# Four reorderings and two blocks of constant matmuls in the two-layer part of a fused Trainium2 kernel

## What is computed

```python
h = rms_norm_2(x, norm_pre)
proj = h @ w_in
y_sb = flat(stick_breaking(heads(sb_q), heads(sb_k), heads(sb_v)))
h_ml = mlstm(...); y_ml = flat(head_norm(h_ml)) * sigmoid(ml_o)
y_gm = spatial_gating(gelu(gm_u), gelu(gm_v), ...)
y_rt = flat(head_norm(retention(rotary(rt_q), rotary(rt_k), rt_v)))
y_xa = flat(memory_attention(heads(xa_q), heads(mem_k), heads(mem_v)))
ys = stack([y_sb*silu(sb_z), y_ml*silu(ml_z), y_gm*silu(gm_z), y_rt*silu(rt_z), y_xa*silu(xa_z)])
up = einsum('bsnw,nwd->bsnd', ys, w_up)
merged = sum(sigmoid(gates) * up, axis=branches)
return x + rms_norm_2(merged @ w_out, norm_post)
```

## Time and profile before

| | |
|---|---|
| median of 3 runs | 2201.73 us (2200.91 to 2202.25) |
| the profiled execution, own time | 2199.61 us |
| its span, first to last instruction | 2197.8 us |
| TensorE busy | 1866.3 us, 85% of the span |
| VectorE busy | 1035.7 us, 47% |
| ScalarE busy | 407.9 us, 19% |
| mean granted clock of TensorE | 0.942 of full |
| moved by DMA | 595.02 MB, mean 271 GB/s |

### The profile page before, as it was taken

The page is one execution under the profiler, slowest core; times in us unless marked ns, Lnnn a source line. Parts: engine busy times, 40 slices in busy tenths (PEclk is TensorE's granted clock), DMA queues, the critical chain, the costliest instruction groups (busy, mean ns, idle before and its releaser), DMA issues. The chain is left out here.

```text
span 2197.8 us, 27405 instructions
## 1 busy us (share of the span) xinstructions
PE 1866.3 (85%) x11528; PEld 1162.8 (53%) x11528; DVE 1035.7 (47%) x1612; ACT 407.9 (19%) x787; POOL 0.2 (0%) x4
## 2 busy tenths in 40 slices
PE   8999977758666667766667999989999999989998
PEld 5687733323323333322223897874446898874445
DVE  7858522212112122122222768678663557768662
ACT  1123300000000000000001233223323233223322
POOL 0000000000000000000000000000000000000000
PEclk9999998888988888888998999999999999999999
DMA  7222899999999999999998334454533334454430
GB/s 307 81 77 102 342 434 429 431 430 432 430 431 429 433 430 430 431 429 430 430 433 348 144 130 159 142 222 153 188 121 136 143 127 169 134 194 193 160 147 19
DMA packets 32375, 595.02 MB, mean 271 GB/s; under 512 B 3966, under 2 KB 5248, under 8 KB 7560
## 3 DMA queue, kind: packets, MB, share of 16 engines
q1 hardware_dynamic: 30344, 584.31, 64.7%
q10 hardware_dynamic: 1920, 9.09, 1.3%
HBM read 590.22 MB, written 1.06 MB: 269 GB/s over the span
## 5 line engine op out<-in xcount | busy, mean ns | idle before, releaser
L2289 PE MATMUL ps<-ring,arena 128*32 128x512 f32 x2032 | 285.9, 714 | 156.3 <-DMA ring<-in_w_experts 147.6
L897 PE MATMUL ps<-ring,arena 128*128 128x512 f32 x656 | 286.4, 592 | 0.0
L2289 PEld LDWEIGHTS ps<-ring,arena 128*32 128x32 f32 x2032 | 72.0, 128 | 354.6 <-issue 219.3
L897 PEld LDWEIGHTS ps<-ring,arena 128*128 128x128 f32 x656 | 124.3, 190 | 155.0 <-issue 155.0
L2323 PE MATMUL ps<-ring,arena 128*32 128x256 f32 x2016 | 151.2, 450 | 62.8 <-DMA ring<-in_w_experts 62.1
L713 PE MATMUL ps<-arena,ring 128*128 128x128 f32 x1536 | 183.2, 275 | 2.7 <-issue 1.8
L713 PEld LDWEIGHTS ps<-arena,ring 128*128 128x128 f32 x1536 | 177.3, 192 | 5.4 <-issue 4.0
L2953 DVE COPY arena<-ps 128x256 f32<-128x256 f32 x64 | 27.2, 425 | 273.0 <-PE ps L2323 273.0
L713 PE MATMUL ps<-early,ring 128*128 128x128 f32 x1152 | 137.3, 275 | 2.9 <-DVE ring L1557 2.9
L2323 PEld LDWEIGHTS ps<-ring,arena 128*32 128x32 f32 x2016 | 70.5, 126 | 130.0 <-issue 76.6
L713 PEld LDWEIGHTS ps<-early,ring 128*128 128x128 f32 x1152 | 133.3, 192 | 4.5 <-DVE ring L1557 3.3
(11 more groups left out here) (476 smaller groups left out, 2471.8 us busy)
## 6 DMA issues: line engine op xcount, KB each, us to landing
ring<-in_w_experts SPq DMA_DIRECT2D x88, 4096.0 KB, 23.4
ring<-in_w_layers SPq DMA_DIRECT2D x64, 2048.0 KB, 7.8
ring<-in_w_experts SPq DMA_DIRECT2D x13, 2048.0 KB, 13.4
ring<-in_w_first SPq DMA_DIRECT2D x9, 2048.0 KB, 8.3
early<-in_w_layers SPq DMA_DIRECT2D x6, 2048.0 KB, 7.9
arena<-in_w_mem SPq DMA_DIRECT2D x4, 2048.0 KB, 20.1
ring<-in_w_first SPq DMA_DIRECT2D x4, 512.0 KB, 7.3
early<-in_w_experts SPq DMA_DIRECT2D x1, 2048.0 KB, 25.2
```

The costliest lines, as they stand in the source:

```text
L897: last = pe.matmul(ps[:, bank, :], lhs[:, k, :], rhs[:, k, :], start=(first and k == 0), stop=(k == n - 1), skip_group_check=True)
L2289: last = pe.matmul(ps[CAP * e:CAP * (e + 1), v // 4, :], xg[:, (v % 4) * 2 + k, CAP * e:CAP * (e + 1)], w[:, k, e, :], start=(v % 4 == 0 a ...
```

## The change

- SyncE waits for `in_turned` (both transfers of the rotation landed) before it issues the load of gm_u, in each layer.
- A helper `hold_clock` multiplies the constant matrix of ones by itself, n matmuls of 128x128 into a PSUM bank that nobody reads: 6 behind the last group of experts (bank 0), 2 ahead of layer 0 and 13 ahead of layer 1 (bank 7).
- TensorE's wait for `gm_mix` moves into the loop over the sb heads, behind `run(2)` and the wait for `sb_sp` of head 0.
- VectorE centres ml_v right behind the bound of the ml exponentials, ahead of `run(3)`.
- In the merge, the additions of g22 and u22 and the bound of g22 form `second_sums`. In branch 0 it stands ahead of the sums of the next branch's weights, in the others behind them as before. The bound of g22 now follows the addition of u22 in all five.

```diff
@@ layers_sync @@
                     if i >= RING2:
                         unit_end(i - RING2)
+                        if UNITS[i] == "gm_u":
+                            sp.wait_ge(sem("in_turned"), 32 * (l + 1))
@@ layers_pe @@
+        def hold_clock(pe, bank, n):
+            for _ in range(n):
+                pe.matmul(ps[:, bank, 0:P], ones, ones, start=True, stop=True)
...
+                hold_clock(pe, 7, 13 if l else 2)
                 unit_in(plan.unit_at["gm_v"])
...
                 sb_logits(1)
                 evacuated(pe, job("sb_v", 1))
-                w("gm_mix", 4, 4)
                 for hd in range(NH):
                     run(2)
                     w("sb_sp", NH, hd + 1)
+                    if hd == 0:
+                        w("gm_mix", 4, 4)
@@ layers_dve @@
                 dve.tensor_scalar(wide_flat, wide_flat, 1e18, None, ALU.min).then_inc(sem("ml_qkm"), 1)
+                centre_values("ml_v", ml_v, ml_sum, "ml_vc")
                 run(3)
...
                 run(2)
                 gate_bound("ml_o")
-                centre_values("ml_v", ml_v, ml_sum, "ml_vc")
                 run(2)
...
+                def second_sums(b):
+                    add_product(b, 1, g22, G_BANK[2], "gate_prod", "gate_c", "gate_q")
+                    add_product(b, 1, u22, U_BANK[2], "up_prod", "up_c", "up_q")
+                    bound(b, 1, g22)
...
+                    if b == 0:
+                        second_sums(b)
                     if b + 1 < NBR:
                         gate_difference(b + 1)
                         gate_total(b + 1)
                         up_sums(b + 1)
-                    add_product(b, 1, g22, G_BANK[2], "gate_prod", "gate_c", "gate_q")
-                    bound(b, 1, g22)
-                    add_product(b, 1, u22, U_BANK[2], "up_prod", "up_c", "up_q")
+                    if b:
+                        second_sums(b)
                     gather(b, 1, merged[:, 1, HALF:D], g22, u22)
@@ end of the first part, TensorE @@
             expert_group(pe.snap(more_rounds * NGRP + NGRP - 1), tail=True)
+            hold_clock(pe, 0, 6)
```

More of the change, by code:

```diff
@@ L1539, in layers_dve, with centre_values @@
                     dve.tensor_tensor(y, y, ps[:, 5, 0:SEQ], ALU.mult).then_inc(sem("xa_y"), 1)
+                def centre_values(name, v, sums, done):
+                    for m in range(2):
+                        evacuated(dve, job(name, m))
+                        heads = v[:, m, :].rearrange("p (h n) -> p h n", h=NH)
+                        link(dve.tensor_reduce(sums[:, m, :], heads, AX, ALU.add))
+                        dve.scalar_tensor_tensor(heads, sums[:, m, :].unsqueeze(2).to_broadcast([P, NH, HD]), -1.0 / HD, heads, ALU.mult, ALU.add).then_inc(sem(done), 1)
                 run(2)
@@ L1549, in layers_dve @@
                 gate_bound("ml_o")
-                def centre_values(name, v, sums, done):
-                    for m in range(2):
-                        evacuated(dve, job(name, m))
-                        heads = v[:, m, :].rearrange("p (h n) -> p h n", h=NH)
-                        link(dve.tensor_reduce(sums[:, m, :], heads, AX, ALU.add))
-                        dve.scalar_tensor_tensor(heads, sums[:, m, :].unsqueeze(2).to_broadcast([P, NH, HD]), -1.0 / HD, heads, ALU.mult, ALU.add).then_inc(sem(done), 1)
-                centre_values("ml_v", ml_v, ml_sum, "ml_vc")
                 run(2)
```

## The result

The changed kernel takes 2167.64 us in the median of four runs (2166.91 to 2168.93), the kernel before 2201.32 in the same group (2200.91 to 2202.25). The ratio is 0.9847, with a 95% interval of 0.983 to 0.9864. The direction was right, and the time is 5.9 us under the 2173.5 of the forecast and 2.4 us under the low end of its range. So the gain is 32 to 34 us.

A forecast was written before the change was run, and what follows sets the result against it. TensorE, busy 85% of the span, was taken as the bound, gains coming from its waits and half clock. 15.9 + 2.9 + 1.8 + 6.0 + 1.6 = 28.2 us off 2199.61 gave 2171.4, plus 2.1: 2173.5 us; range 2170 to 2183.

The forecast's parts named there:

- The rotation: In front of L755 in both layers: TensorE's wait and the half clock behind it go, 15.9 us together.
- The landing: Rotation's two transfers, issued by ScalarE: both landed 7.8 us after the first issue, at 1418.5.
- The margin in front of L755: Layer 0's first rt scores: L1611 ends at 1437.7, just ahead of TensorE's arrival at 1438.06; 0.4 us to spare.
- upper bound of 12.4 us: Rotation's two transfers: the longest they might take alone, as long as now beside the load of gm_u.
- Rival 3: Rotation's transfers need 12.4 us by themselves, so the 15.9 us stay; result 2189.4 us, chance 0.05.
- rival 1: Rotation only partly freed, TensorE still waiting 1 to 4 us a layer; result about 2176 to 2183 us, chance 0.14.
- The values of ml: In front of L713, ml branch: VectorE's earlier centring of ml_v removes the whole wait for L1557, 2.9 us.
- the wait for gm_mix: In front of L713, sb heads: 3.7 us of products before the wait remove it in both layers, 1.8 us.
- The merge: In front of L897: moved sums remove 4.3 us of waits and layer 0's half clock of 1.7 us; 6.0 us.
- the last branch: Merge's end: the new order of bound and addition delays a sigmoid, costing 0 to 0.5 us a layer.
- The constants: Layer starts: held clock returns 1.7 us in layer 0, less 0.1 us cost; nothing to win in layer 1.
- The offset: Whole kernel: the median of runs lies 2.1 us above the profiled execution, so that was added to 2171.4.

## Why the prediction was right and wrong

**The rotation** was right in mechanism and size: 15.9 forecast, 16.2 by the trace, 17 to 18 by the runs. The landing was forecast 7.8 us behind the first issue, from the row of a load of twice the bytes, and came at 6.8 to 7.9. The margin in front of L755 was put at 0.4 us and was a little too wide: where the landing took 7.9 us, some 0.25 us of waiting are back in layer 0, where by the forecast none would be up to 8.2. The prediction's upper bound of 12.4 us counts from each transfer's own issue; from the first one, as its 7.8 does, its own rows give 13.87. On that count the transfers take 12.9 to 13.9 us beside the load (eight passes in four traces) and 6.8 to 7.9 behind the new wait. Rival 3 is refuted by that, and of rival 1 only the 0.25 us are left. The rule of taking turns that the prediction cites from the Trainium skill (DMA: Bandwidth & Descriptors, "Queues, rings and completion order") fits these two figures; the turns themselves no trace here shows.

**The values of ml and the wait for gm_mix** were 2.9 and 1.8 forecast and are 3.2 and 2.1. The idle time was right, and the 0.16 us that each pause costs beyond its idle time was missing.

**The merge** was 6.0 forecast and is 4.7 for the two waits and 1.8 for the clock in that pair of traces; the runs give 6.5 for the moved sums alone. No wait took their place. By all traces the merge gains 2.44 us in each layer, and the half clock behind its pause, put at 1.7 us from one trace, comes in four of ten passes, so 1.4 us on average for the two layers. The 0 to 0.5 us that the last branch might have lost are not there.

**The constants** are the step that failed. "Layer 1 started at full clock (13.97 us for 32 instructions), so there is nothing to win" was read from one execution. Three of the four other traces without the thirteen lose 1.5 to 1.7 us there and one 2.9, and the 1.7 us put for layer 0 is near the low end of what is lost there (1.4 to 3.1 us). The block was put at 1.6 us. It is worth 3.8 us by the average of the traces, 3.3 by the runs when it is added alone, and 4.7 or 5.8 when it is taken back. The prediction had both facts in its hands, a pause of 3.10 us without loss and one of 2.17 us with it, and took one of them for the rule instead of a chance.

**The offset** is a second step that failed. The forecast added 2.1 us, by which the median of the runs lay above the profiled execution of the kernel before. In the changed kernel the profiled execution and its median differ by 0.2 us. A possible reading is that the 2.1 us were clock lost in most executions but not in the profiled one, and that the constants and the removed pauses do away with such losses; the second execution of the kernel before lost 2.9 us at layer 1's start, and its own time was 2202.06 us. It is not shown: each execution's mean clock is on record, and over 66 runs of the kernel before it goes with the time only weakly (correlation -0.40). Nor was 2201.73 the usual time. The seventy runs have a median of 2200.94, 1.3 us above the profiled execution.

**The sum.** Forecast 2171.4 for the profiled execution, measured 2167.41, so 4.0 us too high: 1.6 of them lie ahead of the layers, 2.4 in the layers, made of small shares (0.3 in each of the rotation, ml and gm_mix, 0.5 in the merge, 0.4 at L750, 0.5 unassigned). With the 1.9 us of the offset this is the whole 5.9 us. In this pair the constants at layer 1 gave nothing, so the profiled executions alone would have hidden that error. Over all runs and traces the account is another. Of the 5.9 us, 0.8 are the median of 2201.73 that the forecast started from (2200.94 over seventy runs), and 1.0 is the first group of the changed kernel (2167.64 against 2168.67 over sixteen). That leaves 4.1 us between the forecast gain of 28.2 and the long-run gain of 32.3: 2.2 for the constants (3.8 instead of 1.6), 1.3 for eight pauses at 0.16, 0.4 at L750, 0.2 in the rest of the merge, less 0.3 for the clock behind the merge's pause. That is 3.8 us, and the constants are the largest share. The range was too narrow for the 9.4 us over which single runs of the kernel before spread; a low end near 2166 would have followed from taking 3 us at each border as possible.

**The start of the layers**, at 1189.97 and 1190.70 us in the two traces before and at 1186.08 to 1188.94 in the four after, is not explained. Kernels without the constants stand on both sides (1188.40 with the wait alone, 1191.73 without the constants), as do kernels with them (1191.39 without the thirteen). Ten traces come from kernels that don't differ ahead of the layers (with the six constants, nothing else changed there), and they lie between 1186.08 and 1191.39. So the 1.6 us of the profiled pair can't be told apart from the spread of the executions.

## What to carry to other kernels

Ask of a small transfer on the chain whether a larger load that nobody waits for soon is issued at the same moment, and put the load behind it: one wait on the queue brought 17 us here, and its margin decides how much. Price a pause of TensorE by its idle time, by a small extra (0.16 us here) and by a chance of half clock behind it, taken over several executions rather than read off one. Constant matmuls in such a pause held the clock here when they filled it, and cost nearly their full duration (2.7 of 2.84 us) when they stood a step beside it, so read their place from the trace before timing them.

## What was unexpected

- The same pause of 3.10 us lowered the clock in four of five executions: the 32 instructions behind it took 13.97 us in one and 15.5 to 16.9 in the others. The pause at layer 0's start cost 1.4 to 3.1 us in five executions of the same work. The Trainium skill (TensorE: Matmul & The Clock Gate, "What's actually happening") says that the moment at which the clock changes isn't tied to the kernel and varies from run to run; these rows agree. The same page's section "HAM oscillation — how this bites in real kernels" warns of idle gaps above a certain length; here half clock followed a pause of 2.17 us in four of ten passes and one of 0.96 us in twelve of seventeen, so that a short pause is not safe by its length.
- Constants don't hold the clock always: with all eight in place one of thirteen traces started layer 0 at half clock (15.67 us for 32 instructions). There 1.63 us of the barrier remain between the six and the two.
- Two transfers of 512 KB from SBUF to SBUF have landed, by VectorE's start, 6.8 to 7.9 us after the first issue when no load runs beside them, and 12.9 to 13.9 us after it beside a load of 2 MB. In layer 0 the shorter time came as 6.9 to 7.0 or as 7.9 us and nothing between; why is open.
